# First layer's convolution and query projections: one 512-column product for the high and low activations, with ScalarE and VectorE adding the halves

## The reference, cut to what matters

```python
n = rms_norm(x, attn_norm_g)
proj = n @ w_in
(g_qkv, g_lr, g_out, nq, kc, vc, ks, vs, kw, vw, ng) = jnp.split(proj, offsets, axis=-1)
g_qkv = jax.nn.silu(causal_short_conv(g_qkv, gla_conv_w))
...
def causal_short_conv(u, w):
    s = u.shape[1]
    up = jnp.pad(u, ((0, 0), (CONV_WIDTH - 1, 0), (0, 0)))
    return sum(up[:, i:i + s] * w[i] for i in range(CONV_WIDTH))
```

## Time and profile before

| | before |
|---|---|
| median of 3 runs | 2039.32 us (2038.13 to 2041.28) |
| the profiled execution: its time, its span | 2041.16 us, 2039.4 us |
| TensorE busy | 1994.4 us (98%) |
| VectorE busy | 1611.3 us (79%) |
| ScalarE busy | 933.2 us (46%) |
| GpSimd busy | 171.3 us (8%) |
| TensorE clock granted, mean | 0.991 |
| DMA, mean over the span | 213 GB/s |

### The profile page before, as it was taken

How to read it: one execution, slowest core, us unless ns; L and a number is a source line. 1 busy time by engine, 2 the same in 40 slices (tenths; PEclk the granted TensorE clock), 3 DMA queues, 4 the chain that set the end, 5 groups by cost and what they waited for, 6 DMA issues and landing times.

```text
span 2039.4 us, 37067 instructions
## 1 busy us (share of the span) xinstructions
PE 1994.4 (98%) x13680; PEld 1830.0 (90%) x13680; DVE 1611.3 (79%) x2166; ACT 933.2 (46%) x1326; POOL 171.3 (8%) x263
## 2 busy tenths in 40 slices
PE   7999999999999999999999999999999997999998
PEld 7998898899888998889988899888789996899998
DVE  6986676658888988889889888778887777677754
ACT  6543345645444334443344455245463444444442
POOL 0000000011000000000011111011100120000021
PEclk9999999999999999999999999999999998999999
DMA  7553554346777887777888865676647772668653
GB/s 235 166 164 126 179 173 135 101 158 207 234 230 235 276 301 234 235 238 261 270 282 295 296 221 189 199 258 207 203 151 240 269 272 93 194 206 277 200 186 124
DMA packets 121148, 434.46 MB, mean 213 GB/s; under 512 B 13248, under 2 KB 15680, under 8 KB 120784
## 3 DMA queue, kind: packets, MB, share of 16 engines
q1 hardware_dynamic: 92240, 328.11, 48.9%
q0 software_dynamic: 28800, 104.87, 15.5%
HBM read 430.83 MB, written 2.10 MB: 212 GB/s over the span
## 4 chain that ended last, share of the span: by engine, by line
PE 84%; DVE 11%; DMA 2%; issue 2%; ACT 1%; SPq 0%; DVEq 0%; POOL 0%; POOLq 0%; ACTq 0%
PE ps L611 21%; PE ps L598 12%; PE ps L600 12%; PE ps L599 12%; PE ps L612 11%; DVE w_lo L1587 4%; PE ps L732 2%; DMA side<-w_side 2%; PE ps L1073 1%; PE ps L1083 1%; PE ps L678 1%; PE ps L680 1%; PE ps L679 1%; DVE mod_sum L1604 1%; PE ps L786 1%
## 5 line engine op out<-in xcount | busy, mean ns | idle before, releaser
L611 PE MATMUL ps<-ba_act,w_hi 128*128 128x512 f32 x2240 | 795.6, 400 | 7.3 <-DVE ba_act L1679 3.8
L1203 ACT ACTIVATE w_hi<-raw 128x1024 fp32r<-128x1024 f32 x610 | 622.4, 1053 | 356.7 <-PE ps L600 294.3
L1587 DVE TENSOR_TENSOR w_lo<-raw,w_hi 128x1024 fp32r<-128x1024 f32 x610 | 732.6, 1242 | 52.9 <-ACT w_hi L1203 50.8
L598 PE MATMUL ps<-ba_act,w_hi 128*128 128x256 f32 x2448 | 700.2, 286 | 7.7 <-DVE w_lo L1587 5.9
L599 PE MATMUL ps<-ba_act,w_hi 128*128 128x256 f32 x2448 | 694.1, 284 | 0.0
L600 PE MATMUL ps<-ba_act,w_lo 128*128 128x256 f32 x2448 | 694.1, 284 | 0.0
L612 PE MATMUL ps<-ba_act,w_lo 128*128 128x256 f32 x2240 | 625.5, 279 | 0.0
L611 PEld LDWEIGHTS ps<-ba_act,w_hi 128*128 128x128 f32 x2240 | 421.3, 188 | 113.5 <-issue 7.5
L598 PEld LDWEIGHTS ps<-ba_act,w_hi 128*128 128x128 f32 x2448 | 471.3, 193 | 9.8 <-DVE w_lo L1587 4.5
L599 PEld LDWEIGHTS ps<-ba_act,w_hi 128*128 128x128 f32 x2448 | 471.5, 193 | 0.3 <-issue 0.2
L600 PEld LDWEIGHTS ps<-ba_act,w_lo 128*128 128x128 f32 x2448 | 471.2, 192 | 0.0
(11 more groups left out here) (333 smaller groups left out, 1610.6 us busy)
## 6 DMA issues: line engine op xcount, KB each, us to landing
raw<-w_main SPq DMA_DIRECT2D x610, 512.0 KB, 4.4
side<-w_side POOLq DMA_DIRECT2D x200, 512.0 KB, 4.5
x_tok<-x_in SPq DMA_DIRECT2D x4, 512.0 KB, 7.5
ctx_tok<-ctx_tok SPq DMA_DIRECT2D x1, 2048.0 KB, 11.6
y_out<-res SPq DMA_DIRECT2D x4, 384.0 KB, 3.1
table<-counts_tab SPq DMA_DIRECT2D x1, 512.0 KB, 12.9
y_out<-res SPq DMA_DIRECT2D x2, 256.0 KB, 3.0
cons<-cons_in SPq DMA_DIRECT2D x1, 478.0 KB, 11.3
```

Of the source, the lines that this page charges most:

```text
L598: pe.matmul(out_ap, wh, act_hi[:, kt, :], start=first and n == 0, stop=False)
L611: pe.matmul(ps[:, bank, :], wh, act[:, kt, :, :], start=first and b == 0, stop=False)
L1203: act.activation(w_hi[:, slot, :], raw[:, slot, :], ACT.Copy).then_inc(hi_ready, 1)
L1587: dve.tensor_tensor(w_lo[:, slot, :], raw[:, slot, :], w_hi[:, slot, :].bitcast(F32), ALU.subtract)\
```

## The change

`conv` and `nq` join the list `JOINT`. Their 24 steps take `joint_products` with `a_act` in place of `half_products`. ScalarE copies the low half of each step into the place of the result (`pr`), and VectorE adds the high half before it multiplies by `rstd`: in `conv` by an added instruction into `x_u`, in `nq` by `scaled_sum_read` in place of `scaled_read`.

```diff
-JOINT = ("gout", "nkv", "up0", "up1", "up2", "up2b", "ev_q", "ev_q2", "od_u")
+JOINT = ("conv", "gout", "nkv", "nq", "up0", "up1", "up2", "up2b", "ev_q", "ev_q2", "od_u")
...
-            run("conv", (a_hi, a_lo), chain=chain)
+            run("conv", a_act, chain=chain)
             for stage in ("gout", "nkv"):
                 run(stage, a_act, chain=chain)
-            run("nq", (a_hi, a_lo), chain=chain)
+            run("nq", a_act, chain=chain)
...
-            for stage in ("last", "conv"):
-                ahead(stage, chain=chain)
+            ahead("last", chain=chain)
+            ahead("conv", chain=chain, low=lambda k: pr[:, k, :])
...
-            for stage in ("nq", "outg", "outn"):
+            ahead("nq", chain=chain, low=lambda k: pr[:, NQ + k, :])
+            for stage in ("outg", "outn"):
                 ahead(stage, chain=chain)
...
                 v = x_u[:, k % 2:k % 2 + 1, :]
-                dve.tensor_tensor(v, u, rstd_row, ALU.mult).then_inc(conv, 1)
+                dve.wait_ge(S("low_out"), low_outs("conv", k))
+                then(dve.tensor_tensor(v, u, y, ALU.add))
+                dve.tensor_tensor(v, v, rstd_row, ALU.mult).then_inc(conv, 1)
...
-            reading("nq", scaled_read(NQ), chain=chain)
+            reading("nq", scaled_sum_read("nq", NQ), chain=chain)
```

## The result

| | before | change |
|---|---|---|
| median, 5 runs each | 2039.32 us (2038.13 to 2041.37) | 2048.72 us (2046.90 to 2051.59) |
| ratio, 95% interval | | 1.0048 [1.0035, 1.0061] |
| the profiled execution: time, span | 2041.16, 2039.4 us | 2046.90, 2045.2 us |
| TensorE clock granted, mean | 0.991 | 0.994 |

The change costs 9.4 us. The forecast was 7.3, that is 2046.6 us in all, and 2048.72 lies in the stated range of 2042.0 to 2051.5.

What follows compares the result with a forecast made beforehand. TensorE and VectorE are both near their limit in `conv`; in `nq` a circle through VectorE and ScalarE makes TensorE wait. 2039.3 + 5.1 (`conv`) + 2.2 (`nq`) = 2046.6 us; own range 2043.5 to 2050, stated range 2042 to 2051.5.

Steps and rivals of the forecast that it cites:

- What bounds conv: In `conv`, TensorE busy 96.83 and VectorE 90.03 of 99.00 us, both near their limit; with the change VectorE sets the pace.
- The late read: In `conv`, from a late read's start to the step after next: 3.65 us before, 3.65 + 0.45 = 4.1 us with the change.
- TensorE's waits in conv: Waits for `w_lo` at steps 7, 8 and 9, some 4 us in all; for `g_q` and `g_kd` 2 to 3 us more.
- The term for conv: Step 17 starts 5.1 us later: 5.85 us of added VectorE work less 0.7 of filled pauses; bounds 2.9 to 6.5.
- Between, nothing: In the stages between `conv` and `nq`, already joint, the 5.1 us delay is carried on with nothing added or made up.
- The term for nq: In `nq`, copy and longer read delay `k_cmp`, `w_lo`, `q_rs` and `pt_second`: net 2.2 us, bounds -1.0 to 8.0.
- TensorE's gain of 0.12 us a step: Joint steps take 5.72 us against 5.84, 2.9 us over 24 steps if nothing else is late; shortens nothing in `conv`.
- The signs of being wrong: TensorE's `conv` waits for VectorE under 2 us, joint steps over 5.84 us without a wait, or delay shrinking after step 60.
- Nothing stalls: Rival: VectorE's 6.7 us of pauses in `conv` take in the added work, only the gain is left: 2036.4 us, chance 0.10.
- half of it: Rival: `conv` stalls at the low bound, 2.9 us, and those of `nq` cost 0.6: 2042.8 us, chance 0.13.
- The circle goes on: Rival: every `nq` step pays copy, wait and add, 8.0 us, lateness passing on to `outg`: 2052.4 us, chance 0.12.

Runs made afterwards that it cites:

- e4: The kernel before, all separate, with one more VectorE product in each read of `conv`: `conv` +5.83 us with one clock fall, median +4.4 us, ratio 1.0030.
- e3: The change in `conv` only, without VectorE's add but with ScalarE's copies and the wait: `conv` +1.71 us, median +2.4 us against before, ratio 1.0010.
- e12: The change plus 8 filling matmuls on TensorE at step 43: `nq` +2.04 us without a clock fall, median +8.6 us against before, ratio 1.0039.
- e7: The change in `nq` only, without ScalarE's copies, VectorE adding `rstd` instead: `nq` +2.26 us with one clock fall, median +1.7 us against before, ratio 1.0008.
- e6: The change in `conv` only, without ScalarE's copies, VectorE adding `rstd` instead: `conv` +5.06 us with one clock fall, median +6.2 us against before, ratio 1.0030.
- e11: The kernel before, unedited, executed once more for a second trace: 2036.87 us.
- e13: The changed kernel, unedited, executed once more for a second trace: 2048.36 us, `conv` +7.10 and `nq` +3.70 us against before, a clock fall in each.
- e8: The change plus 18 filling matmuls on TensorE at step 43: `nq` +4.08 us without a clock fall, median +9.6 us against before, ratio 1.0048.
- e9: The change in `conv` only, ScalarE making the first tap and VectorE half of `w_lo` earlier: `conv` +3.76 us, median +4.6 us against before, ratio 1.0019.

## Why the prediction was right, point by point

- **What bounds conv** held. VectorE is the engine that sets the end once 0.42 us a step are added: e4 shows it without any other edit.
- **The late read.** I had 4.1 us from the start of a late read to the step after next. The timeline of VectorE in the change, read of step 7, `w_lo` of step 9, and the reads of steps 9, 12 and 15:

```profile
73.73 0.42 DVE L1753 TENSOR_TENSOR x_u<-ps,pr 128x256 f32<-128x256 f32 x1
...
76.47 2.35 DVE L1588 TENSOR_TENSOR w_lo<-raw,w_hi 128x1024 fp32r<-128x1024 f32 x2
...
84.28 0.42 DVE L1753 TENSOR_TENSOR x_u<-ps,pr 128x256 f32<-128x256 f32 x1 [0.44 <-ACT pr L1210]
...
108.92 0.42 DVE L1753 TENSOR_TENSOR x_u<-ps,pr 128x256 f32<-128x256 f32 x1 [1.11 <-ACT pr L1210]
...
129.19 0.43 DVE L1753 TENSOR_TENSOR x_u<-ps,pr 128x256 f32<-128x256 f32 x1 [0.20 <-ACT pr L1210]
```

  The read of step 7 starts at 73.73 and TensorE starts step 9 at 77.84, 4.11 us later. From read to `w_lo` it is 2.74 us, in the earlier trace rows 2.28: the 0.45 of an added instruction is there. The pauses before the reads of steps 9, 12 and 15 are 0.44, 1.11 and 0.20, laid out as 0.3, 1.1 and 0.1; the one before step 4 is 0.24, laid out as 0.4.
- **TensorE's waits in conv.** For `w_lo` 3.5 us (about 4), 1.31 at step 8 and 1.56 at step 9 (1.6 and 1.8); for `g_q` and `g_kd` 5.4 in place of 1.9, 3.5 more, above the 2 to 3 that I had.
- **The term for conv** was 5.1 and is 5.65, within its bounds of 2.9 and 6.5. Its two causes were weighed wrongly inside it: I gave the instruction 5.85 us less 0.7 of filled pauses, and the copy nothing but 0.4 us at reads that are not late. The add costs 3.9 on top of the copy, and e3 shows 1.7 for the copy alone. That the sum came out near is partly luck.
- **Between, nothing** is exact: 154.82 us from step 17 to 37 in both.
- **The term for nq** was 2.2 and is 2.04 in e12, without a fall. The four waits are the four that I named. The three old ones are longer by 1.8 us together (4.7 in place of 2.9), where I had 3 to 4, and the new one adds 1.0. `q_rs` (0.9 in place of 0.6) and `pt_second` (1.9 in place of 1.4) grew less than the 2.0 and 2.3 of lateness; the waits before had made TensorE itself late by then. Copy and add as causes stood in the prediction, and e7 bears out the copy: some two thirds of the 2.04 go with it.
- **TensorE's gain of 0.12 us a step.** Steps 4 and 15 hold no wait in either trace, and each takes 5.65 us in the change and 5.76 before, from its first matmul to the next step's: 0.11 us less. From the zero to step 3 it is 10.52 against 10.82. By the page "TensorE: Matmul & The Clock Gate" of the Trainium skill, section "Wait — 56ns, not 53.3ns?", an estimate would have been 16 x 2.5 ns = 0.04 us a step; these steps do not agree with it, and the rows did better. That the gain shortens nothing in `conv`, as I had it, is not quite borne out: e6 against e4 lets some 0.8 of the 1.9 us arrive.
- **The missing term** is the fall of the clock, 1.7 us in `nq` in both executions of the change and 1.5 in `conv` in the second. I had costed a wait of TensorE at its own length. 5.65 + 2.04 = 7.7 is what stalls alone make, 0.4 from the forecast; with the falls it is 9.4 and 10.8. That the median still fell into the range is owed to the width of the range. What I wrote for the traces at step 45 (7.3 later) was 8.58, and is 9.42 with the zeros laid on each other. The span forecast for the profile, 2046.7 us, was too high (2045.2) although the two stages cost more than forecast: the trace of before that it was reckoned from is the slowest behind step 45.
- **The signs of being wrong.** TensorE's waits for VectorE in `conv` stay over 2 us (8.9), and a joint step without a wait takes less than 5.84 us (5.65). The third, a delay that shrinks after step 60, did show in the first pair of traces (2.8 us less), and only e11 makes it the spread of executions.
- **The rivals.** "Nothing stalls" and "half of it" are out by the rows. "The circle goes on" named 2052.4 us and would have explained more than was found: behind step 44 nothing is added, and `nq` pays 2.0 us of stalls, not 8.0.

## What to carry to other kernels

A saving on the busiest engine can be lost whole where a second engine has 90% of the stage: ask first what the edit adds there, and cost it by the number of steps up to the next place at which that engine has a pause. A hand-over through a third engine costs even where that engine is idle, because the reader starts later: 1.7 to 2.1 us in the 16 steps of `conv`, and some 1.3 us in the 8 of `nq`. And a wait on TensorE may have to be costed at more than its length: here a fall of the clock behind it added 1.2 to 1.7 us, in some executions and not in others, so it belongs into the range and not into the sum.

## What the runs showed that I had not expected

- A fall of the granted clock to 0.50 for 3.4 us, in `nq` of the change behind a wait of TensorE of 1.87 us. Such falls are worth 1.2 to 1.7 us. The same code had it in one execution and not in another (`conv` in the change and in e13).
- By TensorE's own step marks, two executions of the same kernel agree to 0.01 us over 330 us when no such fall lies between (before and e11). What differs beside is the start-up (3.2 us between the traces) and the stretch behind step 45 (3.4 us).
- With the wait at step 43 filled with matmuls of constants there was no fall behind it (e8, e12), and 8 of them (e12) cost the work behind them no time.
- Taking the first tap off VectorE (e9) brought 1.9 us, a new wait of ScalarE for VectorE of 11.8 us, and one the other way of 9.9 in place of 6.6; no form with a joint `conv` came down to the kernel before.
